# Start addresses of the split activations, chosen layer by layer, in a four-layer fp32 kernel on one core

## The reference, cut to what matters

```
# layers 0 and 1 (D = 1024, D_FF = 2816, S = 256)
h = rmsnorm(x, norm1_g[l]) * (1.0 + sc1) + sh1
proj = h @ w_in[l]                      # u_f, q, k, v, g, a_f, a_r: 7 x 1024 columns
y_f = fourier_mix(u_f) @ w_fourier[l]
y_r = retention_branch(q, k, v, g) @ w_ret[l]
x = x + g1 * ((sigmoid(a_f) * y_f + sigmoid(a_r) * y_r) @ w_out[l])
h = rmsnorm(x, norm2_g[l]) * (1.0 + sc2) + sh2
a, b = split(conv3(h @ ffn_up[l]))      # 2 x 2816 columns
x = x + g2 * ((gelu(a) * b) @ ffn_down[l])

# layers 2 and 3 (x: 256 tokens, ctx: 256 tokens; only layer 2 updates ctx)
a = modulate(rms_norm(h, norm1_g[l]), sh1, sc1)
p, u, vs, q, k, v, gl = split(a @ w_in[l])
y = gp * (pool @ w_po) + gs * (sgu @ w_so) + ga * (attn @ w_ao)
h = h + g1 * (y @ w_o[l])
h = h + g2 * (square(relu(modulate(rms_norm(h, norm2_g[l]), sh2, sc2) @ w_ff1[l])) @ w_ff2[l])
```

## The kernel before, in words

| buffer | address | modulo 512 |
|---|---|---|
| `stage`, `w_hi`, `w_lo`, `X` | 16512, 36992, 53376, 69760 | 128 |
| `h_hi`, `h_lo` | 86144, 102528 | 128 |
| temporary buffers (`sq`, `tt`, `conv`, `relu`, `sc` and others) | from 133952 on | 320 |
| phase buffers at `ph` (`q1`, `u_hi`, `u_lo`, `r_hi`, `r_lo`, `f_hi`, `f_lo`, `b_hi`, `b_lo` and others) | from 154560 on | 448 |

## Time and profile before

### The profile page before, as it was taken

One profiled execution on the slowest core, in us unless ns is written; L12 is line 12 of the kernel. 1 busy time (PEld: TensorE's weight loads), 2 busy tenths in 40 slices (PEclk: granted clock), 3 DMA queues, 4 the chain that ended last, 5 costly groups with the idle time before them and its releaser, 6 DMA issues.

```text
span 2116.1 us, 36942 instructions
## 1 busy us (share of the span) xinstructions
PE 2080.5 (98%) x14236; PEld 1916.5 (91%) x14236; DVE 1496.3 (71%) x2161; ACT 987.6 (47%) x1501; POOL 392.7 (19%) x288
## 2 busy tenths in 40 slices
PE   8999999999999999999999999999999989999998
PEld 7999999999999999999877888888888988999998
DVE  5876888877777899978988524897533466866554
ACT  4444456544445566553245523432232245755453
POOL 0330203210511213224101102130010031121020
PEclk8999999999999999999999999999999999999999
DMA  7876767686675666664544322456632244564552
GB/s 285 293 253 199 253 221 250 239 288 214 213 239 197 212 199 216 197 233 132 184 165 146 108 85 87 137 182 229 197 101 91 81 158 160 203 214 160 183 186 100
DMA packets 109594, 396.36 MB, mean 187 GB/s; under 512 B 12408, under 2 KB 13056, under 8 KB 109056
## 3 DMA queue, kind: packets, MB, share of 16 engines
q1 hardware_dynamic: 108160, 389.99, 54.7%
q0 software_dynamic: 1280, 4.20, 0.6%
HBM read 393.09 MB, written 1.05 MB: 186 GB/s over the span
## 4 chain that ended last, share of the span: by engine, by line
PE 84%; DVE 11%; DMA 2%; ACT 2%; issue 1%; POOL 0%; DVEq 0%; SPq 0%; POOLq 0%; ACTq 0%
PE bank L486 21%; PE bank L488 21%; PE bank L487 21%; DVE w_lo L1435 5%; PE bank L587 2%; PE bank L585 2%; PE bank L586 2%; DMA stage<-in_stream 1%; PE bank L661 1%; PE bank L658 1%; DVE stage L1456 1%; PE bank L606 1%; DVE rstd L1453 1%; PE bank L509 1%; PE bank L877 1%
## 5 line engine op out<-in xcount | busy, mean ns | idle before, releaser
L1435 DVE TENSOR_TENSOR w_lo<-stage,w_hi 128x1024 fp32r<-128x1024 f32 x536 | 705.0, 1330 | 457.2 <-ACT w_hi L1004 456.9
L1004 ACT ACTIVATE w_hi<-stage 128x1024 fp32r<-128x1024 f32 x536 | 565.7, 1059 | 849.0 <-PE bank L488 599.9
L486 PE MATMUL bank<-h_hi,w_hi 128*128 128x256 f32 (+1 forms) x2560 | 788.5, 308 | 6.8 <-DVE w_lo L1435 4.1
L487 PE MATMUL bank<-h_lo,w_hi 128*128 128x256 f32 (+1 forms) x2560 | 782.9, 306 | 0.0
L488 PE MATMUL bank<-h_hi,w_lo 128*128 128x256 f32 (+1 forms) x2560 | 782.9, 306 | 0.0
L486 PEld LDWEIGHTS bank<-h_hi,w_hi 128*128 128x128 f32 x2560 | 489.8, 191 | 36.5 <-DVE w_lo L1435 7.4
L487 PEld LDWEIGHTS bank<-h_lo,w_hi 128*128 128x128 f32 x2560 | 489.8, 191 | 21.6 <-issue 0.5
L488 PEld LDWEIGHTS bank<-h_hi,w_lo 128*128 128x128 f32 x2560 | 489.7, 191 | 21.5
L1456 DVE SCALAR_TENSOR_TENSOR stage<-stage,cvec 128x1024 f32<-128x1024 f32 x188 | 253.8, 1351 | 4.2 <-DMA stage<-in_stream 1.7
L486 PE MATMUL bank<-f_hi,w_hi 128*128 128x256 f32 (+1 forms) x448 | 147.3, 329 | 0.0
L488 PE MATMUL bank<-f_hi,w_lo 128*128 128x256 f32 (+1 forms) x448 | 146.7, 327 | 0.0
(11 more groups left out here) (254 smaller groups left out, 3272.2 us busy)
## 6 DMA issues: line engine op xcount, KB each, us to landing
stage<-in_stream SPq DMA_DIRECT2D x728, 512.0 KB, 4.3
bias<-in_bias POOLq DMA_DIRECT2D x16, 256.0 KB, 3.2
X<-in_x SPq DMA_DIRECT2D x2, 1024.0 KB, 7.0
cvec<-in_cvec SPq DMA_DIRECT2D x3, 512.0 KB, 4.1
decay<-in_decay SPq DMA_DIRECT2D x1, 1024.0 KB, 5.4
out<-X SPq DMA_DIRECT2D x4, 256.0 KB, 2.1
rope<-in_rope SPq DMA_DIRECT2D x2, 256.0 KB, 4.9
wsgu<-in_wsgu SPq DMA_DIRECT2D x2, 256.0 KB
```

Source lines behind the costliest of these rows:

```text
L486: mm(out, w_hi[:, slot, w], xh[:, c, 0:T], start=first, stop=False)
L487: mm(out, w_hi[:, slot, w], xl[:, c, 0:T], start=False, stop=False)
L1004: A(w_hi[:, m % NR, :], stage[:, n % NS, :], ACT.Copy).then_inc(hi_ready, 1)
L1435: do(V.tensor_tensor(w_lo[:, m % NR, :], stage[:, n % NS, :], w_hi[:, m % NR, :].bitcast(F32), ALU.subtract), unit_done, done_value(n))
```

## The change

The change gives addresses. A new helper `operands` makes one view of a buffer for each different address and returns a list by layer, so that the code says `h_hi[L]` instead of `h_hi`. The views of one buffer overlap; the engines' instructions, their order, their shapes and their semaphores stay as they are. `half_sum`, `ccol`, `vsum`, `vmean`, `MUL` and `idle` are placed ahead of `h` now.

```
         X = sb("X", [P, 2, DC, S])
-        h_hi = sb("h_hi", [P, DC, T2], F32R)
-        h_lo = sb("h_lo", [P, DC, T2], F32R)
-        cols = sb("cols", [P, NCOL])
-        cvec = sb("cvec", [P, 2, D])
+        edge = where[0]
...
+        def operands(name, shape, at):
+            tiles = {a: sb(name if n == 0 else f"{name}_{n}", shape, F32R, a) for n, a in enumerate(sorted(set(at)))}
+            return [tiles[a] for a in at]
+
+        HBYTES = DC * T2 * 4
+        h_at = [edge + off for off in (448, 448, 512, 448)]
+        assert where[0] <= min(h_at)
+        h_hi = operands("h_hi", [P, DC, T2], h_at)
+        h_lo = operands("h_lo", [P, DC, T2], [at + HBYTES for at in h_at])
+        where[0] = max(h_at) + 2 * HBYTES
...
-        ph = where[0]
+        ph = where[0] + 64
+        top = ph + 64
...
-        u_hi = sb("u_hi", [P, FC, S], F32R, ph)
-        u_lo = sb("u_lo", [P, FC, S], F32R, ph + 22 * KB)
+        u_at = [ph + off for off in (0, 0)]
+        u_hi = operands("u_hi", [P, FC, S], u_at)
+        u_lo = operands("u_lo", [P, FC, S], [at + 22 * KB for at in u_at])
...
-        b_hi = sb("b_hi", [P, 4, T2], F32R, ph + 40 * KB)
-        b_lo = sb("b_lo", [P, 4, T2], F32R, ph + 48 * KB)
+        b_at = [ph + 40 * KB + off for off in (0, 0, 64, 0)]
+        b_hi = operands("b_hi", [P, 4, T2], b_at)
+        b_lo = operands("b_lo", [P, 4, T2], [at + 8 * KB for at in b_at])
...
-        f_hi = sb("f_hi", [P, 16, T2], F32R, ph)
-        f_lo = sb("f_lo", [P, 16, T2], F32R, ph + 32 * KB)
+        f_at = [ph + off for off in (0, 0, 64, 0)]
+        f_hi = operands("f_hi", [P, 16, T2], f_at)
+        f_lo = operands("f_lo", [P, 16, T2], [at + 32 * KB for at in f_at])
...
-                        feature_block(L, f"d{half}1", f_hi, f_lo, T, nothing)
+                        feature_block(L, f"d{half}1", f_hi[L], f_lo[L], T, nothing)
```

More of the change, by code:

```diff
@@ L232, in program @@
         vmean = sb("vmean", [P, 2, 2, 2])
+        MUL = sb("MUL", [P, 2, 2, 2, DC])
+        idle = sb("idle", [1, 16])
+        def operands(name, shape, at):
[7 more added lines that the diff above has]
+        where[0] = max(h_at) + 2 * HBYTES
+        cols = sb("cols", [P, NCOL])
+        cvec = sb("cvec", [P, 2, D])
         MOD = sb("MOD", [P, 2, 2, MODC])
-        MUL = sb("MUL", [P, 2, 2, 2, DC])
         eps = sb("eps", [P, 1])
@@ L237, in program @@
         ones = sb("ones", [P, P])
-        idle = sb("idle", [1, 16])
         rstd = sb("rstd", [P, T2])
@@ L831, in _ @@
                     pe.wait_ge(s["loaded2"], 64)
-                feature_block(L, "k", h_hi, h_lo, T2, lambda i: pe.wait_ge(s["h_ready"], HREADY[L, "n1" if L == 2 else "c1"] + DC),
+                feature_block(L, "k", h_hi[L], h_lo[L], T2, lambda i: pe.wait_ge(s["h_ready"], HREADY[L, "n1" if L == 2 else "c1"] + DC),
                               before={3: lambda: rotated("rq", q2, "q")})
@@ L858, in pool_and_mix @@
                         close_group(last, g)
-                token_block(L, "v", h_hi, h_lo, nothing)
+                token_block(L, "v", h_hi[L], h_lo[L], nothing)
                 pool_and_mix()
@@ L937, in run @@
                     if name[0] == "g":
-                        feature_block(L, name, h_hi, h_lo, T, nothing)
+                        feature_block(L, name, h_hi[L], h_lo[L], T, nothing)
                     elif name[0] == "p":
@@ L972, in _ @@
                         if L == 2 and b == 0:
-                            half_passes(L, "f0", h_hi, h_lo, [(x_part, (2, "n2")), (ctx_part, (2, "c2"))],
+                            half_passes(L, "f0", h_hi[L], h_lo[L], [(x_part, (2, "n2")), (ctx_part, (2, "c2"))],
                                         hooks={(0, 2, 0): lambda: norm_sums(2, "c2")})
                         else:
-                            feature_block(L, f"f{b}", h_hi, h_lo, T, h_ready(L, "n2") if b == 0 else nothing,
+                            feature_block(L, f"f{b}", h_hi[L], h_lo[L], T, h_ready(L, "n2") if b == 0 else nothing,
                                           after_norm=None if b else (L, "n2"))
                     base = 32 * (L - 2) + 16 * half
-                    feature_block(L, f"d{half}0", f_hi, f_lo, T, count("ff_ready", base))
+                    feature_block(L, f"d{half}0", f_hi[L], f_lo[L], T, count("ff_ready", base))
                     if L == 2 and half:
-                        split_units(L, "d11", f_hi, f_lo, 4, hooks={(1, 5, 0): lambda: norm_sums(3, "n1")})
+                        split_units(L, "d11", f_hi[L], f_lo[L], 4, hooks={(1, 5, 0): lambda: norm_sums(3, "n1")})
                     else:
-                        feature_block(L, f"d{half}1", f_hi, f_lo, T, nothing)
+                        feature_block(L, f"d{half}1", f_hi[L], f_lo[L], T, nothing)
                 if L == 3:
@@ L1057, in highs @@
                     act.wait_ge(s["t_ready"], base + c + 1)
-                    A(h_hi[:, c, tok], tt[:, c % 4, tok], ACT.Identity,
+                    A(h_hi[layer][:, c, tok], tt[:, c % 4, tok], ACT.Identity,
                       bias=MOD[:, layer % 2, v, shift + c:shift + c + 1]).then_inc(s["hhi_ready"], 1)
@@ L1902, in _ @@
                 dve.wait_ge(s["aohi_ready"], 4 * (L - 1))
-                take(V.tensor_tensor(b_lo[:, PAIRS - 1, 0:T], bank_of(g)[:, 0:T], b_hi[:, PAIRS - 1, 0:T].bitcast(F32),
+                take(V.tensor_tensor(b_lo[L][:, PAIRS - 1, 0:T], bank_of(g)[:, 0:T], b_hi[L][:, PAIRS - 1, 0:T].bitcast(F32),
                                      ALU.subtract), g)
```

98 lines of the change are left out of this document (49 added, 49 removed).

## The result

The changed kernel is faster by 0.9%: 2100.38 us (median of four runs, 2091.97 to 2105.86) against 2116.98 us before, ratio 0.9914 with a 95% interval of 0.9900 to 0.9928. Run again later beside other runs of before it had 2101.41 us (five runs, 2100.45 to 2104.15), ratio 0.9935 (0.9921 to 0.9948). The first profiled execution took 2098.63 us, 1.8 us more than its span. So 1.8 us do lie around the span, and with them the span of before, 2116.1 us, goes with the run of 2117.84 us and not with the median that it happened to equal. That is why the two spans differ by 19.3 us and the medians by 16.6.

The account below looks back on a forecast made before the run. PE, busy 98% of the span, was taken as the bound, through the pitch of its matmuls. 14.4 + 0 + 0.6 - 0.2 - 2.4 = 12.4 us off 2116.1 gave 2103.7 us; own range 2098 to 2109, widened to 2091 to 2111.

Parts of the forecast that it names:

- That an address sets the pitch: Feature-block matmuls: remainder 448 is 2.2 ns better than 128 at 256 columns, 1.8 ns worse at 512; no address part 0.07.
- The pitch at 64: 256-column matmuls moved to 64: taken as 118.0 ns, like 448; 6528 of h gain 14.4 us.
- The rival of a better 64: 256-column matmuls: 64 beats 448 by 1.1 ns, h gains 21.5 us, time 2095.6 us; chance 0.27.
- The text's own test: Trace after: a pitch at 64 outside 117.5 to 118.5 ns would show the forecast's size wrong.
- The end from below: h at 256 columns: all 13.5 ns beyond the columns gone, 88 us gained; called an end no row comes near.
- Layer 2: b and f from 448 to 128: 1.4 us gained at 512 columns, 0.8 lost at 256, net 0.6 gained.
- `h` at 512 columns in layer 3: Block k, three lines of 32, from 128 to 64: costs 96 x 1.8 = 0.2 us.
- Places where `h` stands: Line 585, its neighbours and line 658, weights moving: taken as nothing; some 530 matmuls by 2 ns are 1 us.
- Layers 0 and 1: 4800 h matmuls of 256 columns gain 2.2 ns each; 2.4 us written off where VectorE limits PE.
- VectorE's rival: VectorE takes over in layers 0 and 1: gains up to 957 us halved, time 2106.6 us; no separate chance given.
- Layer 3: 1728 h matmuls of 256 columns gain 2.2 ns each, 512-column h loses 0.2 us, u, b and f 0.
- The sign: Whole kernel: faster 0.83, same 0.07, slower 0.10; a common pitch at 64 above 119.6 ns would make it lose.

Follow-up runs that it names:

- the second execution: Changed kernel, nothing altered, profiled again in the later rerun beside runs of before: span 2098.7 us; that rerun's median 2101.41 us, ratio 0.9935.
- the stretches alone: Kernels computing nothing of the reference, only stretches of 96 feature-block matmuls with operand addresses varied; at 256 columns, weights and rows at 128 gave 120.0 ns.

## Why the prediction was right, and where it wasn't

- **That an address sets the pitch:** right, shown with everything else idle and with the weights moved instead. But the text read the moving row's own remainder modulo 512 as what counts. It is the difference to the weights' remainder, modulo 256. The trace of before could not tell: its weights stood at 128 throughout.
- **The pitch at 64:** the step that was mis-sized. 118.0 ns was taken from 448 as the nearest row; against the weights at 128 that is difference 64, and the new addresses have 192, another layout. 64 has that pitch (117.8) and a shorter one, 113.3. The rival of a better 64 took 116.9. Over the 4515 short and 4208 long ones of the first profiled execution the mean is 115.5 (4515 x 113.3 + 4208 x 117.8, by 8723), but no stretch has it. The text's own test, a pitch outside 117.5 to 118.5, struck, and so did two others: a difference where the weights move, and PE idle time behind `w_lo` that grows by more than 3 us. The end from below, all 13.5 ns of the pitch beyond its columns, was not as far off as it was called: the short pitch takes away 6.9 of them, where the sum gave 2.2.
- **Layer 2:** right in its pitches, 226.9 ns for `f` at 512 columns and 120.1 at 256 as written; 0.6 us forecast and 0.6 measured, but 2.5 us in the second execution, 1.7 of the difference by a higher granted clock, so the exact hit is luck.
- **`h` at 512 columns in layer 3:** the sign right, the size not: 402 ns in place of 396, 233.3 ns of pitch instead of 228.7, 0.6 us instead of 0.2.
- **Places where `h` stands:** taken as nothing, bounded by 1 us. 395 ns in place of 392 for the 64 of one line; by the starts of 96 such matmuls in layers 0 and 1 the pitch went from 228.0 to 230.0 ns, and 2 ns over all 530 would be 1.1 us, about the bound.
- **Layers 0 and 1:** 10.6 us less 2.4 forecast, 5.5 and 9.4 measured in two executions. In the first execution PE's idle time there grew by 6.9 us (17.2 to 24.1) and the granted clock cost 6.9 us more (13.7 against 6.8), so the shorter pitch itself had brought 5.5 + 6.9 + 6.9 = 19.3 us, and 13.8 of them were given back where 2.4 were written off (1.7 of the 13.8 by the clock of the first 31 us, which differs between executions anyway). VectorE's rival was right in its place, and the clock was missing from it. In 762:891 PE's idle time was to grow by about 1 us; in the same blocks, 756:886 of the changed kernel, it grew from 1.7 to 4.8.
- **Layer 3:** 3.6 us forecast, 13.2 and 5.5 measured; the short pitch again.

So 12.4 us came from a sum in which the gain per matmul was too small and so was what was written off, and 16.6 us was measured. The two misses offset each other in part, and that the time came so near is luck to that extent. The sign rested on the part that was right: an address with a pitch no worse than 448's. The rule of the Trainium skill (SBUF — State Buffer, Who interferes with whom), by which TensorE has two independent read ports, one for the moving operand and one for the weight load, doesn't fit in its effect: with all other engines idle, the pitch goes from 113.3 to 120.0 ns with the distance between the addresses of the two operands. That it never waits on anyone is said there of the other engines, and is not touched by this. Which part of the chip does it, no run here shows. The spacing of N/2.4 + 2.5 ns, which the prediction took from the Trainium skill, is by the cited section that of a matmul by itself; for streams with weight loads, as here, the section gives other spacings, which the prediction left out.

Open are the cause of the two rhythms, why `w_lo` at 0 leaves only the short one (shown as a fact in 26 stretches and in one kernel), and why stretches entered from `h` at 120.0 ns without a pause had one pitch only, 113.3 at difference 192 and 117.8 at difference 64. That last was seen in the real kernels and not tried alone.

## What to carry to other kernels

Where TensorE bounds and loads weights for each matmul, compare the pitch of equal shapes over different buffers; if it differs, lay the moving and the standing operand apart by a chosen distance modulo 256, and choose it by the width. A single profile of such a kernel shows one draw of the pitches: stretches must be compared one by one, and several runs be made. And ask which engine is next before counting a gain per instruction: here VectorE, 96% busy in 762:891, took back part of the gain in layers 0 and 1.

## What was not expected of the hardware

- One program, one clock, one load, and two pitches, 113.3 and 117.8 ns, each held for over a thousand matmuls and, in the stretches alone, one or the other behind equal pauses.
- At 256 columns equal remainders (modulo 256) of rows and weights are the worst of the multiples of 64 (120.0 ns), and at 512 columns the best (226.7 against up to 233.3).
- A wait of 2.8 us of PE stood in 64 us with a mean granted clock of 0.95 in one kernel, and in 64 us with 1.00 in another.
